# Modulation of the normed input on three engines: prompt columns on VectorE and ScalarE, sample columns on GpSimd

## The reference, cut to what matters

```python
mod = jax.nn.silu(c) @ p['w_ada'] + p['b_ada']
sh1, sc1, g1, sh2, sc2, g2 = jnp.split(mod, 6, axis=-1)
h = _rmsnorm(x, p['norm_mix_w']) * (1.0 + sc1[:, None]) + sh1[:, None]
mix, new_states = _mixer(h, lru_conv, lru_h, dn_conv, dn_S, reset_first, p)
x = x + g1[:, None] * mix
h = _rmsnorm(x, p['norm_ffn_w']) * (1.0 + sc2[:, None]) + sh2[:, None]
x = x + g2[:, None] * _peer(h, p)
```

## Time and profile before

| | |
|---|---|
| median of three runs | 4352.23 us (4347.91 to 4360.71) |
| the profiled execution | 4374.36 us, span 4372.5 us |
| busy share of the span: PE, DVE, ACT, POOL | 85%, 69%, 34%, 48% |
| first modulation stage | about 332 to 366 us after the span's start |
| second modulation stage | about 1699 to 1733 us |

### The profile page before, as it was taken

The page is one execution under the profiler, slowest core; times in us unless marked ns, Lnnn a source line. Parts: engine busy times, 40 slices in busy tenths (PEclk is TensorE's granted clock), DMA queues, the critical chain, the costliest instruction groups (busy, mean ns, idle before and its releaser), DMA issues. The chain is left out here.

```text
span 4372.5 us, 65820 instructions
## 1 busy us (share of the span) xinstructions
PE 3735.8 (85%) x24298; PEld 3475.5 (79%) x24298; DVE 3022.4 (69%) x4531; ACT 1476.1 (34%) x1889; POOL 2100.9 (48%) x1164
## 2 busy tenths in 40 slices
PE   6876999998896898987669999999988888888887
PEld 3336888988886797987569898889988888888886
DVE  5777645455545223898967777777878888888886
ACT  5665343434442113222323333333332222222222
POOL 2433222222224233324346777677766767666662
PEclk9997999999997998998889999999999999999898
DMA  8981222222222123223369999999999999999994
GB/s 308 355 319 51 83 79 83 73 79 71 68 69 97 54 96 110 82 71 106 144 269 389 414 406 405 393 402 409 399 376 378 394 387 402 388 400 399 408 403 154
DMA packets 253104, 1090.19 MB, mean 249 GB/s; under 512 B 25353, under 2 KB 78857, under 8 KB 172297
## 3 DMA queue, kind: packets, MB, share of 16 engines
q1 hardware_dynamic: 167440, 543.60, 33.8%
q0 software_dynamic: 73728, 536.90, 30.1%
q10 hardware_dynamic: 11776, 7.52, 0.6%
HBM read 1047.54 MB, written 40.40 MB: 249 GB/s over the span
## 5 line engine op out<-in xcount | busy, mean ns | idle before, releaser
L248 POOL TENSOR_TENSOR wlo<-raw,whi 128x1024 fp32r<-128x1024 f32 x551 | 1342.5, 2440 | 1470.8 <-ACT whi L244 1465.4
L244 ACT CAST whi<-raw 128x1024 fp32r<-128x1024 f32 x670 | 697.0, 1049 | 1242.0 <-DMA raw<-in_u 541.0
L263 PE MATMUL gps<-hi_d,whi 128*128 128x320 f32 x2048 | 663.1, 324 | 161.5 <-POOL wlo L248 108.0
L2110 PE MATMUL gps<-chi,whi 128*128 128x320 f32 x2048 | 651.1, 318 | 101.6 <-DVE outacc L2239 85.0
L263 PE MATMUL gps<-lo_d,whi 128*128 128x320 f32 x2048 | 653.6, 319 | 0.0
L263 PE MATMUL gps<-hi_d,wlo 128*128 128x320 f32 x2048 | 652.8, 319 | 0.0
L2110 PE MATMUL gps<-clo,whi 128*128 128x320 f32 x2048 | 640.7, 313 | 0.0
L2110 PE MATMUL gps<-chi,wlo 128*128 128x320 f32 x2048 | 640.6, 313 | 0.0
L2197 DVE SCALAR_TENSOR_TENSOR dps<-ring,coef,dps 128x2048 f32<-128x2048 f32 x252 | 591.6, 2348 | 6.3 <-DMA ring<-in_v_rows,spi 1.6
L2184 DVE CUSTOM_DVE_ANT_0 ring<-ring,dps 128x2048 f32<-128x2048 f32 x256 | 581.9, 2278 | 0.0
L263 PEld LDWEIGHTS gps<-hi_d,whi 128*128 128x128 f32 x2048 | 404.0, 197 | 179.0 <-POOL wlo L248 118.1
(11 more groups left out here) (388 smaller groups left out, 6026.6 us busy)
## 6 DMA issues: line engine op xcount, KB each, us to landing
raw<-in_u SPq DMA_DIRECT2D x256, 512.0 KB, 10.6
raw<-in_v SPq DMA_DIRECT2D x256, 512.0 KB, 7.8
wada<-in_w_ada SPq DMA_DIRECT2D x96, 1024.0 KB, 6.5
raw<-in_w_in SPq DMA_DIRECT2D x96, 512.0 KB, 3.5
gateD<-gst SPq DMA_DIRECT2D x8, 2560.0 KB, 7.5
gate<-gateD SPq DMA_DIRECT2D x32, 640.0 KB, 17.3
raw<-in_w_out SPq DMA_DIRECT2D x32, 512.0 KB, 3.6
raw<-in_w_q SPq DMA_DIRECT2D x32, 512.0 KB, 4.0
```

Of the source, the lines that this page charges most:

```text
L244: act.copy(whi[:, k.slot, :], raw_of(k)).then_inc(W.hi, 1)
L248: pool.tensor_tensor(wlo[:, k.slot, :], raw_of(k), whi[:, k.slot, :].bitcast(F32), ALU.subtract).then_inc(W.lo, 1)
L263: m = pe.matmul(gps[:, bank, 0:DT], w, x[:, kt, :], start=(kt == 0 and n == 0), stop=(kt == KT - 1 and n == 2))
L2110: m = pe.matmul(gps[:, 2 + dt, 0:DT], w[:, slot, cols], x[:, buf, c, :], start=(c == 0 and n == 0), stop=(c == NG - 1 and n == 2))
```

## The change

The prompt columns and the sample columns are taken apart. VectorE makes the product of source, scale and `rstd` for the 512 prompt columns in one instruction with three operands; ScalarE adds the shift while it rounds, and writes `hi` directly; VectorE makes the remainder as (`tmp` + shift) - `hi`, now for all 16 k. The 64 sample columns go through GpSimd: product with `rstd`, times scale, plus shift, and after ScalarE's rounding copy of these columns the remainder. TensorE waits for both remainders. Two of the waits that VectorE had on its own results go, and GpSimd gets two per k on its own.

```diff
             def dve_part(dve):
...
                     if k < KT:
-                        t = tmp[:, k % 4, :]
                         if k >= 4:
-                            dve.wait_ge(*lo_count(k - 4))
-                        dve.tensor_tensor(t, src[:, k, :], rstd[:, :], ALU.mult).then_inc(M.normed, 1)
-                        dve.wait_ge(M.normed, before + k + 1)
-                        ch(dve.tensor_tensor(samples(t), samples(t),
-                                             bc(amod[:, k, 1:NC].unsqueeze(2), [P, NB, NS]), ALU.mult))
-                        dve.tensor_tensor(samples(t), samples(t), bc(modT[:, shift + k, 1:NC].unsqueeze(2), [P, NB, NS]),
-                                          ALU.add).then_inc(M.h, 1)
-                    if k - 2 in on_dve:
-                        dve.wait_ge(M.hi, before + per * (k - 1))
-                        rest(dve, k - 2, M.lo_dve)
+                            dve.wait_ge(M.lo_dve, lo_before + n_lo * (k - 3))
+                        dve.scalar_tensor_tensor(tmp[:, k % 4, 0:TP], src[:, k, 0:TP], amod[:, k, 0:1], rstd[:, 0:TP],
+                                                 ALU.mult, ALU.mult).then_inc(M.normed, 1)
+                    if k >= 2:
+                        j = k - 2
+                        dve.wait_ge(M.hi, hi_before + n_hi * j + n_lo)
+                        for hi, lo, at, cols in prompt:
+                            dve.scalar_tensor_tensor(lo[:, j, at], tmp[:, j % 4, cols], modT[:, shift + j, 0:1],
+                                                     hi[:, j, at].bitcast(F32), ALU.add, ALU.subtract
+                                                     ).then_inc(M.lo_dve, 1)
 
             def act_part(act):
                 act.wait_ge(M.scales, before // KT + 1)
                 for k in range(KT):
-                    t = tmp[:, k % 4, :]
                     act.wait_ge(M.normed, before + k + 1)
-                    act.activation(t[:, 0:TP], t[:, 0:TP], ACT.Identity, bias=modT[:, shift + k, 0:1],
-                                   scale=amod[:, k, 0:1]).then_inc(M.prompt, 1)
-                    act.wait_ge(M.prompt, before + k + 1)
+                    for hi, lo, at, cols in prompt:
+                        act.activation(hi[:, k, at], tmp[:, k % 4, cols], ACT.Identity, bias=modT[:, shift + k, 0:1],
+                                       scale=1.0).then_inc(M.hi, 1)
                     act.wait_ge(M.h, before + k + 1)
-                    for hi, lo, cols in layout:
-                        act.copy(hi[:, k, :], t[:, cols]).then_inc(M.hi, 1)
+                    act.copy(s_hi[:, k, s_at], tmp[:, k % 4, TP:T]).then_inc(M.hi, 1)
 
             def pool_part(pool):
-                for k in range(KT):
-                    if k not in on_dve:
-                        pool.wait_ge(M.hi, before + per * (k + 1))
-                        rest(pool, k, M.lo_pool)
+                pool.wait_ge(M.scales, before // KT + 1)
+                for k in range(KT + 1):
+                    if k < KT:
+                        t = tmp[:, k % 4, :]
+                        if k >= 4:
+                            pool.wait_ge(M.lo_pool, before + k - 3)
+                        pool.tensor_tensor(t[:, TP:T], src[:, k, TP:T], rstd[:, TP:T], ALU.mult).then_inc(M.sample, 1)
+                        pool.wait_ge(M.sample, 2 * (before + k) + 1)
+                        pool.tensor_tensor(samples(t), samples(t), bc(amod[:, k, 1:NC].unsqueeze(2), [P, NB, NS]),
+                                           ALU.mult).then_inc(M.sample, 1)
+                        pool.wait_ge(M.sample, 2 * (before + k) + 2)
+                        pool.tensor_tensor(samples(t), samples(t), bc(modT[:, shift + k, 1:NC].unsqueeze(2), [P, NB, NS]),
+                                           ALU.add).then_inc(M.h, 1)
+                    if k >= 1:
+                        j = k - 1
+                        pool.wait_ge(M.hi, hi_before + n_hi * (j + 1))
+                        pool.tensor_tensor(s_lo[:, j, s_at], tmp[:, j % 4, TP:T], s_hi[:, j, s_at].bitcast(F32),
+                                           ALU.subtract).then_inc(M.lo_pool, 1)
 
             def pe_part(pe, k):
 
-                pe.wait_ge(*lo_count(k))
+                pe.wait_ge(M.lo_dve, lo_before + n_lo * (k + 1))
+                pe.wait_ge(M.lo_pool, before + k + 1)
```

More of the change, by code:

```diff
@@ L499, in build, with modulate @@
         M.h, M.hi, M.lo_dve, M.lo_pool = sems(stack, "mod_h", "mod_hi", "mod_lo_dve", "mod_lo_pool")
[L500 to L509, removed]
-                for hi, lo, cols in layout:
[L511 to L518, removed]
+        M.scales, M.normed, M.sample = sems(stack, "mod_scales", "mod_normed", "mod_sample")
+        def modulate(before, hi_before, lo_before, src, rstd, amod, tmp, weight, shift, scale, layout):
+            prompt = [(hi, lo, slice(0, min(cols.stop, TP) - cols.start), slice(cols.start, min(cols.stop, TP)))
+                      for hi, lo, cols in layout]
+            s_hi, s_lo, s_cols = layout[-1]
+            s_at = slice(TP - s_cols.start, T - s_cols.start)
+            n_lo = len(prompt)
+            n_hi = n_lo + 1
             def dve_part(dve):
@@ L559, in pe_part @@
             def pe_part(pe, k):
-                pe.wait_ge(*lo_count(k))
+                pe.wait_ge(M.lo_dve, lo_before + n_lo * (k + 1))
+                pe.wait_ge(M.lo_pool, before + k + 1)
             return dve_part, act_part, pool_part, pe_part
-        first_h = modulate(0, xT, rB, amod, tmp, normw[0], 0, KT, one_layout)
+        first_h = modulate(0, 0, 0, xT, rB, amod, tmp, normw[0], 0, KT, one_layout)
         with ExitStack() as c2:
@@ L1486, in _ @@
                     ch.leave(KT // 2 - 1)
-        second_h = modulate(KT, x1T, rB2, amod2, tmp2, normw[1], 3 * KT, 4 * KT, two_layouts)
+        second_h = modulate(KT, 2 * KT, KT, x1T, rB2, amod2, tmp2, normw[1], 3 * KT, 4 * KT, two_layouts)
         N7 = N5 + 4 * H
```

## The result

The changed kernel takes 4394.44 us (median of four runs, 4383.56 to 4416.0), the kernel before beside it 4355.02. The ratio is 1.0083, 95% interval 1.0053 to 1.0113: slower by 39 us, where I had forecast no change and a range that ended at 4374.

What follows compares the result with a forecast made beforehand. VectorE was taken to pace the two modulation stages, about 2.0 us per k; GpSimd with turns would replace it at 2.12 and 1.99. Stage shifts +1.6 and -0.8 sum to +0.8 us on 4352.23: 4353.0, range 4342 to 4374.

Steps and rivals of the forecast that it cites:

- The price of GpSimd's small instructions: Modulation stages: each 64-column GpSimd instruction takes 0.32 us, between 0.135 and 0.73; each 0.1 us is 12.8 us.
- The dear rival: Modulation stages: GpSimd's small instructions have a fixed part; at 0.50 us each, 23 us longer, 4376; chance 0.14.
- The turns: Modulation stages: each VectorE instruction between GpSimd's costs GpSimd 0.39 us (512 columns) or 0.13 (256); periods 2.12 and 1.99.
- rival on the turns: Modulation stages: turns cost whole instructions, 28 us more, chance 0.06; or small instructions fit into gaps, 17 us less, 0.13.
- VectorE's three-operand instructions: Modulation stages: VectorE's new instructions take 0.67 us (512 columns) and 0.40 (256); alone it needs 1.33 and 1.47 per k.
- the bounds of 0.81 and 0.26: Modulation stages: ScalarE takes at most 0.81 us per 512 columns plus 0.26 for the 64-column copy, 1.07 per k.
- The ends: After each stage's last add: ScalarE's copy and rounding, 1.3 us, precede line 248; start shifts +1.6 and -0.8 us.
- Its additional wait, for GpSimd's counter, covers the same k: TensorE in the modulation stages: needs 1.44 us per k, under 2.0, so the added wait was given no cost.
- assumption that nothing else moves: Outside the two modulation stages: no change of more than a few us; shifts at line 248 reach the end in full.
- slower by over 0.3%: Whole kernel: outcome from dear small GpSimd instructions or turns costing whole instructions; chance 0.20.

Runs made afterwards that it cites:

- With the loops in place: Changed kernel with 68 instructions more in TensorE's program, at its start (1.0002) or ahead of the expert loops (1.0001), against the kernel before.

## Why the prediction was wrong

*The price of GpSimd's small instructions*: right. 0.32 us was taken for 64 columns; undisturbed they take 0.313 to 0.317, and 0.295 and 0.353 with the repeated operand. The dear rival (from 0.42 us on) is out.

*The turns*: right in price. Beside VectorE GpSimd's records are stretched to 0.76, by 0.45 us, and by 0.39 in the median of all that are; 0.39 was taken. Its period is 2.15 us per k in the first stage and 1.98 in the second, for 2.12 and 1.99. Neither rival on the turns came: the stages are neither 28 us longer nor 17 us shorter. But the reason given for the price, that a turn does not last for the whole record, was wrong. In the kernel after, all 66 of GpSimd's records that took over 0.4 us begin 0.07 to 0.44 us behind the start of a VectorE record and end 0.15 to 0.18 us behind its end; one such pair:

```profile
348.00 0.75 DVE L527 SCALAR_TENSOR_TENSOR act_lo<-tmp,modT,act_hi 128x512 fp32r<-128x512 f32 x1 [0.39 <-ACT act_hi L536]
348.15 0.76 POOL L550 TENSOR_TENSOR tmp<-tmp,amod 128x64 f32<-128x64 f32 x1
```

VectorE ends at 348.75, GpSimd at 348.91. So GpSimd stands until VectorE's instruction has ended, and pays no more than what is left of that when its own begins. Where in VectorE's record it begins was not part of the sum; that the price held is in part luck. The Trainium skill (SBUF — State Buffer, section Who interferes with whom) has it that the first to start holds the shared ports for its whole instruction; the trace agrees, which the prediction denied.

*VectorE's three-operand instructions*: 0.67 and 0.40 us were taken, 0.75 to 0.79 and 0.51 measured. It is not the pace, so that costs little. *ScalarE*: 0.72 and 0.246, under the bounds of 0.81 and 0.26.

*The ends*: line 248 begins 1.30 us behind the last add (363.94 to 365.24), as forecast. The stages: +2.5 us for +1.6, -0.7 for -0.8; together +1.8 for +0.8. VectorE waits for ScalarE's `hi` 13 times in the first stage, as forecast, but only 7 in the second. With the loops in place the program is as fast as before, 1.0002 and 1.0001, which is the forecast of 4353.

*The step that failed* is the sentence on TensorE, "Its additional wait, for GpSimd's counter, covers the same k", with the "assumption that nothing else moves". The wait was priced as time, and as such it costs nothing. It was not counted as 28 instructions in the longest program of the kernel. I compared engines by the instructions that do work, and those with a wait only are not among them. What came in its place is the refetch: 27 packets more, nine in each of three turns, 23.8 us in the first expert loop. The trace of before had the signs: queue 8 with 105 packets for a program of some 60 blocks, and 45 of them in the loop over the heads. The Trainium skill (Runtime: NRT & Kernel Launch, section Instruction fetch mechanics) says that TensorE's instruction memory is 128 KiB, filled in blocks of 16 KiB or 256 instructions, the next one fetched while the current one runs. That fits the packets, and eight such blocks fit the edge found here, a loop of seven and the block ahead. That section calls the cost of crossing a block mostly hidden, and warns that a taken branch stalls where its target is not in the current window of two pages. The stall agrees where a loop touches eight blocks; the window of two does not, since a loop of seven brings no packets in its later turns.

*The rivals*: slower by over 0.3% had 0.20, for causes that were not it.

Why a stall of 3 to 4 us costs 8 a turn in the first expert loop and 3 in the third can be read from the profiles. Steps between the starts of two products of 0.2 to 0.32 us are counted as lower clock, longer ones as waits. In the first loop a refetched turn spends 5.3 us more in waits than a turn at hand (means of six and eight profiles) and 2.6 more at the lower clock; that is the 7.9. The waits are more than the stall because later ones grow with it: over the three turns PE's wait for `wlo` from GpSimd, in the kernel before and with the wait written twice, is

```profile
PE gps L263 <- POOL wlo L248: 16.1, 10, 2.1
```

```profile
PE gps L263 <- POOL wlo L248: 20.8, 10, 3.6
```

In the third loop the stall mostly takes the place of a wait that stood there anyway, for `outacc`; the kernel before, then with 138 instructions ahead of the expert loops:

```profile
PE gps L2110 <- DVE outacc L2239: 44.4, 24, 3.9
```

```profile
PE gps L2110 <- DVE outacc L2241: 28.9, 21, 4.4
...
PE gps L2110 <- issue: 15.5, 7, 3.8
PE gps L2110 <- DVE clo L2213: 12.2, 3, 4.2
```

That TensorE is busier in the first loop than in the third (92% for 85%, 707 of 830 us, in the kernel before) is not the reason by itself: over the heads it is busy for 91% (592 of 648 us in the kernel before), and the refetch there costs nothing that shows. Why the waits for `wlo` grow was not tested.

## What to carry to other kernels

On TensorE a loop whose body spans some seven blocks of 256 instructions has an edge: count its blocks, and look at the packets of the instruction queue by loop before and after any edit that adds instructions to that engine, waits included, however far ahead of the loop. No run here tried it on another engine. If packets go up in a loop that the diff doesn't touch, shift the loop by some tens of satisfied waits where the engine idles, and time that beside the edit, or the edit is judged for what its placement did. A shorter body should do better than a shift; that was not tested.

## What was not expected of the hardware

- A loop is refetched whole or not at all: nine packets a turn, from eight instructions on. The branch back then takes 4.5 to 6.6 us in the expert loops, where the DMA engines are busy all the time (DMA share 0.99 to 1.02), and 3.5 to 4.6 over the heads, where the share is 0.23; whether that is the reason was not tested. It takes 0.21 to 0.24 where the body is at hand.
- Satisfied waits are not free when there are many: ahead of the expert loops TensorE's first product came (30.39 - 19.12) / (195 - 90) = 0.107 us later with each instruction past those that its idle time covers.
- A stop of 3.4 us is followed by some 3 us of products at the 1.2 GHz level (0.27 us apart from 2504.18 on, 0.147 again from 2507.38).
